# Heads of the fourth mixer computed already turned, both compressions on one tile, diagonal blocks moved by sums, and a new order for the mixers

## The reference, cut to what matters

```python
def nsa_compress(kv, pos_emb, w1, w2):          # first mixer: for keys, and again for values
    ...
    flat = (blocks + pos_emb.astype(jnp.float32)).reshape(B, G, n, CMP_BLOCK * d)
    return jax.nn.gelu(flat @ w1.astype(jnp.float32)) @ w2.astype(jnp.float32)

def hgrn2_chunkwise(q, k, v, log_f):             # second mixer
    ...
    attn = jnp.sum(qc[:, :, :, None, :] * decay * kc[:, :, None, :, :], axis=-1)

def chunk_attention(x, k_band, v_band, band_valid, w_q, rel_table, w_o):   # fourth mixer
    q = (x @ w_q).reshape(b, nc, CHUNK, B_HEADS, B_HEAD_DIM) * (B_HEAD_DIM ** -0.5)
    ...
    sc = jnp.einsum('bnqhd,bnkhd->bhnqk', q, k_band,
                    preferred_element_type=jnp.float32) + bias[:, None]
```

## Time and profile before

| | us |
|---|---|
| median of 3 runs | 1274.83 |
| lowest and highest | 1274.36, 1276.19 |
| the profiled execution, its own time | 1274.34 |
| its span, first to last instruction | 1272.5 |

### The profile page before, as it was taken

How to read it: one execution, slowest core, us unless ns; L and a number is a source line. 1 busy time by engine, 2 the same in 40 slices (tenths; PEclk the granted TensorE clock), 3 DMA queues, 4 the chain that set the end, 5 groups by cost and what they waited for, 6 DMA issues and landing times.

```text
span 1272.5 us, 20336 instructions
## 1 busy us (share of the span) xinstructions
PE 1256.7 (99%) x7562; PEld 1055.9 (83%) x7562; DVE 501.2 (39%) x1108; ACT 766.1 (60%) x1481; POOL 1029.1 (81%) x874
## 2 busy tenths in 40 slices
PE   8999999999999999999999999999999999999997
PEld 7877888888887887888888888888888888888886
DVE  3575423331168862333105665133203345233302
ACT  7656676654688877666445685365534565366631
POOL 6666789878977568988888877798889887699874
PEclk9999999999999999999999999999999999999999
DMA  8543566656654436666666545677565644567652
GB/s 284 159 133 108 158 209 217 194 166 185 183 163 134 134 94 206 195 187 189 178 194 195 162 150 148 198 213 218 184 196 174 224 149 136 162 215 224 202 171 82
DMA packets 63121, 224.96 MB, mean 177 GB/s; under 512 B 7344, under 2 KB 7984, under 8 KB 63024
## 3 DMA queue, kind: packets, MB, share of 16 engines
q1 hardware_dynamic: 62736, 223.57, 57.1%
q10 hardware_dynamic: 288, 0.10, 0.0%
HBM read 222.59 MB, written 1.05 MB: 176 GB/s over the span
## 4 chain that ended last, share of the span: by engine, by line
PE 94%; DVE 2%; POOL 2%; ACT 2%; DMA 1%; issue 1%; SPq 0%; DVEq 0%; ACTq 0%
PE G L1048 18%; PE G L1049 17%; PE G L1055 17%; PE G L1074 10%; PE A L1074 10%; PE A L1077 5%; PE G L1077 5%; POOL wlo L2328 1%; PE A L1179 1%; PE A L1103 1%; PE A L1215 1%; PE A L1239 1%; DMA X<-in_x 0%; PE A L1339 0%; PE A L1318 0%
## 5 line engine op out<-in xcount | busy, mean ns | idle before, releaser
L2328 POOL TENSOR_TENSOR wlo<-raw,whi 128x256 fp32r<-128x256 f32 (+2 forms) x866 | 1019.6, 1213 | 225.8 <-ACT whi L2028 224.8
L2028 ACT ACTIVATE whi<-raw 128x1024 fp32r<-128x1024 f32 x403 | 422.3, 1057 | 199.6 <-PE G L1055 145.0
L1048 PE MATMUL G<-whi,xx 128*128 128x512 f32 (+1 forms) x560 | 226.0, 404 | 0.5 <-DVE xx L1435 0.3
L1049 PE MATMUL G<-whi,xx 128*128 128x512 f32 (+1 forms) x560 | 217.1, 388 | 0.0
L1055 PE MATMUL G<-wlo,xx 128*128 128x512 f32 (+1 forms) x560 | 171.3, 388 | 0.0
L1074 PE MATMUL G<-xx,whi 128*128 128x512 f32 x576 | 144.7, 393 | 0.0
L1074 PE MATMUL A<-xx,whi 128*128 128x512 f32 x576 | 144.4, 393 | 0.0
L1048 PE MATMUL G<-whi,hh 128*128 128x512 f32 x352 | 137.6, 391 | 0.0
L1049 PE MATMUL G<-whi,hl 128*128 128x512 f32 x352 | 137.2, 390 | 0.0
L1048 PEld LDWEIGHTS G<-whi,xx 128*128 128x128 f32 x560 | 105.3, 188 | 24.9 <-issue 5.5
L1055 PEld LDWEIGHTS G<-wlo,xx 128*128 128x128 f32 x560 | 104.6, 188 | 22.4
(11 more groups left out here) (388 smaller groups left out, 1499.3 us busy)
## 6 DMA issues: line engine op xcount, KB each, us to landing
raw<-in_g SPq DMA_DIRECT2D x88, 512.0 KB, 3.9
raw<-in_u SPq DMA_DIRECT2D x88, 512.0 KB, 4.1
raw<-in_d SPq DMA_DIRECT2D x88, 512.0 KB, 4.0
raw<-in_w_h SPq DMA_DIRECT2D x32, 512.0 KB, 3.6
raw<-in_w_e SPq DMA_DIRECT2D x24, 512.0 KB, 3.9
raw<-in_w_a SPq DMA_DIRECT2D x24, 512.0 KB, 3.6
raw<-in_w_b SPq DMA_DIRECT2D x24, 512.0 KB, 3.7
raw<-in_w_eo SPq DMA_DIRECT2D x8, 512.0 KB, 3.6
```

Of the source, the lines that this page charges most:

```text
L1048: e.matmul(o, sh[:, kt, xs], whi[h][:, ws], start=u.first and j == 0, stop=False)
L1049: e.matmul(o, sl[:, kt, xs], whi[h][:, ws], start=False, stop=False)
L2028: e.activation(whi[c % NH][:, 0:n], raw[c % NR][:, 0:n], ACT.Copy).then_inc(s_hi, 1)
L2328: m = e.tensor_tensor(wlo[c % NH][:, i:j], raw[c % NR][:, i:j], whi[c % NH][:, i:j].bitcast(F), ALU.subtract)
```

## The change

It does five things. (1) The blocks of w_b are ordered v 0, qk 0 to qk 3, v 1, and q and k are computed in sixteen turned units of one chunk each, two heads on the 128 partitions (`turned_heads`); they use two banks in turn, an ACT copy (`QX`) and a DVE add (`QA`) put the halves together in `QTa` or `KTa`, and head n+2 waits for the add of head n. `KT`, `KA`, `KV` and the evictions of q and k leave the fourth mixer, which has 48 units instead of 64. (2) `CA` computes keys on the lower and values on the upper 64 columns of the array, in turn; the GELU runs once on 128 partitions, and `CF` and `CG` are one step each. (3) `DB` and the placing of the position embeddings (`MB`) use a `tensor_reduce` over an axis of one element instead of `tensor_copy`. (4) The side steps of all mixers stand in a new order. (5) In the first mixer the gates' buffer waits for one `CA`, not two.

```diff
+B_ORDER = (("v", 0), ("qk", 0), ("qk", 1), ("qk", 2), ("qk", 3), ("v", 1))
...
+                if st == 6 and B_ORDER[blk][0] == "qk":
+                    for j in range(4):
+                        ((c, kts),), at = feed(name, D, 128, at)
+                        units.append(Unit(st, ("h", 4 * B_ORDER[blk][1] + j), c, 0, kts, 128, 0, True, True))
+                    continue
...
+        def head_bank(n):
+            return G[0][:, 512 * (n % 2):512 * (n % 2) + 512]
+        def head_rest(n):
+            return PJ2[:, n % 2, 256 * (n // 2):256 * (n // 2) + 256]
...
+            def turned_heads(u):
+                _, n = u.blk
+                h, o = u.chunk % NH, head_bank(n)
+                before = B_ORDER.index(("qk", n // 4)) - 1
+                e.wait_ge(s_hi, u.chunk + 1)
+                if n % 4 > 1:
+                    half_added(n - 2)
+                elif B_ORDER[before][0] == "qk":
+                    half_added(4 * B_ORDER[before][1] + 2 + n % 4)
+                else:
+                    evicted(6, before, n % 4)
+                for kt in u.kts:
+                    e.matmul(o[:, :], whi[h][:, 128 * kt:128 * kt + 128], xx[:, kt, :], start=kt == 0, stop=False)
+                e.wait_ge(s_lo, u.chunk + 1)
+                for kt in u.kts:
+                    m = e.matmul(o[:, 0:256], wlo[h][:, 128 * kt:128 * kt + 128], xx[:, kt, 0:256], start=False,
+                                 stop=kt == u.kts[-1])
+                m.then_inc(s_unit, 1)
...
-                    wt = w1c[:, kind, 64 * m:64 * m + 64]
-                    o = e.matmul(tile[0:64, 0:45].rearrange("p (g i) -> p g i", g=3), wt, z, start=m == 0, stop=m == 15)
+                    for kind in range(2):
+                        z = Z[:, 3 * kind:3 * kind + 3, 2 * m:2 * m + 225:16]
+                        o = e.matmul(tile[64 * kind:64 * kind + 64, 0:45].rearrange("p (g i) -> p g i", g=3),
+                                     w1c[:, kind, 64 * m:64 * m + 64], z, start=m == 0, stop=m == 15)
...
-                    m = e.tensor_copy(mixed[rows, :, :, rows], blocks[rows])
+                    m = e.tensor_reduce(mixed[rows, :, :, rows], blocks[rows].unsqueeze(4), X_AX, ALU.add)
...
+            def half_add(key):
+                if j < 2:
+                    e.scalar_tensor_tensor(out=to, in0=head_bank(n)[:, 0:256], scalar=0.125, in1=head_rest(n), op0=ALU.mult,
+                                           op1=ALU.add).then_inc(S["QA"], 1)
+                else:
+                    e.tensor_tensor(to, head_bank(n)[:, 0:256], head_rest(n), ALU.add).then_inc(S["QA"], 1)
...
+            def half_copy(key):
+                _, n = key
+                e.wait_ge(s_unit, ENDS[6, ("h", n), 0])
+                e.activation(head_rest(n), head_bank(n)[:, 256:512], ACT.Copy,
+                             scale=0.125 if n % 4 < 2 else 1.0).then_inc(S["QX"], 1)
```

The new order of the fourth mixer around the turned heads (units 8 to 23), of the second mixer where the diagonal step and the decay products stand, and of the start:

```diff
+8: QX 0; QA 0
...
+12: QX 4; SC 0 0 @1; SC 0 1 @2; QA 4; MK 0 0; MK 0 1; EX 0 0; NW 0 0; LB 2
+13: QX 5; QA 5
+14: QX 6; QA 6; CPA 0 0; TR 0 0; EX 0 1
+15: QX 7; QA 7; AV 0 0
+16: NW 0 1; WH 0 0; QX 8; WL 0 0; SC 1 0 @0; QA 8; TBM 2; SC 1 1 @1; MK 1 0
+17: MK 1 1; TR 0 1; CPA 0 1; CPV 0 1; QX 9; QA 9; EX 1 1; QX 10
+18: LB 3; EX 1 0; QA 10
+19: TR 1 1; QX 11; NW 1 1; QA 11
+20: CPV 1 1; NW 1 0; QX 12; QA 12; WL 0 1; TR 1 0; CPA 1 1
...
-29: H4 0 1; H3 1 0; H4 1 0
-32: H4 1 1; GF 0; FB 2 @2
+30: H4 0 1; H4 1 0; HA 0 1; H3 1 1; H5 0 1; HA 1 0; GB 0 @2; GC 0; EV 3 1; H4 1 1
-35: FD 2; DB 0
+35: DB 0; FD 2
-38: H1 2 0 @1; H2 2 0; FF 2; T1 1 @0; TV 1; EV 4 0; FG 2; EV 4 1; TA 1
+38: H1 2 0 @1; H2 2 0; FF 2; T1 1 @0; TV 1; EV 4 0; FG 2; TA 1; EV 4 1
-42: H1 2 1 @0
+44: H1 2 1 @0; H5 2 0; GF 1; H1 3 1 @1; H1 3 0 @2
...
--1: -XT 0 0; -SQ 0 0; -XH 0 0; HI 0; -XL 0 0; -XT 0 1; LO 0; -XH 0 1; -XT 1 0
+-1: -XT 0 0; -SQ 0 0; -XH 0 0; HI 0; -XL 0 0; -XT 0 1; LO 0; -XT 1 0
-0: HI 1; -XT 1 1; -XL 0 1; -XH 1 0; HI 2
+0: HI 1; -XH 0 1; -XT 1 1; -XL 0 1; -SQ 0 1; HI 2; -XH 1 0
-18: CA 0 @2; CA 1 @0; CB 0; TT 2 @1; CE 0; TC 2; CB 1; EV 2 0; CD 0; CD 1; CE 1; CG 0; MK 0 0 1; MK 1 0 0
+18: CB 0; CE 0; EV 2 0; CD 0; TC 2; CG 0; MK 0 0 1
+19: CA 0 @0; TT 2 @1; QT 0 @2; MK 1 0 0
```

More of the change, by code:

```diff
@@ L139 @@
 A_AT = [(512 * i if kind == "qk" else 2048 + 512 * i, 512) for kind, i in A_ORDER]
-BLOCKS = {0: E_AT, 2: H_AT, 4: A_AT, 6: A_AT}
+B_AT = [(512 * i if kind == "qk" else 2048 + 512 * i, 512) for kind, i in B_ORDER]
+BLOCKS = {0: E_AT, 2: H_AT, 4: A_AT, 6: B_AT}
 QK_BLOCK = [A_ORDER.index(("qk", p)) for p in range(4)]
-V_BLOCK = [A_ORDER.index(("v", i)) for i in range(2)]
+V_BLOCK = {st: [order.index(("v", i)) for i in range(2)] for st, order in ((4, A_ORDER), (6, B_ORDER))}
 H_BLOCK = {pair: i for i, pair in enumerate(H_ORDER)}
@@ L580 @@
 70: RES 0 0; BN 0 0
[L581 removed]
+74: RES 0 1
+82: BN 0 1
 85: TBM 1
@@ new lines @@
+22: QX 14; QA 14
+23: SC 2 0 @0; SC 2 1 @2; QA 15; MK 2 0; QX 15; EX 2 0; MK 2 1; SC 3 0 @1
+24: NW 2 0
+25: EX 2 1; CPA 2 0; MK 3 0
+26: TR 2 0
+27: NW 2 1; EX 3 0; NW 3 0; EV 5 0
+28: CPV 2 1
+29: CPA 2 1; TR 2 1; WL 2 0
+30: EV 5 1; CPA 3 0; WH 2 0
+32: TR 3 0; WH 2 1; WH 3 0
+33: WL 2 1; MK 3 1; AV 2 0; AV 3 0; AV 2 1; SC 3 1 @0; NW 3 1; WL 3 0; RES 0 0
+35: EX 3 1
+42: TR 3 1; CPV 3 1; BN 0 0; RES 1 0; BN 1 0
+43: CPA 3 1; AG 0; WH 3 1; WL 3 1; AV 3 1; AP 0 0
+44: RS 0
+45: AP 1 0; XT 0 0; XH 0 0
@@ L631 @@
+46: XL 0 0
+47: RES 0 1; BN 0 1; XT 1 0
 """,
@@ L1033, in product @@
                         e.wait_ge(S["RO"], nth("RO", u.st, ROTATED[u.st, u.blk - 1], u.t))
+                    elif u.st == 6 and not wide and u.blk > 0:
+                        half_added(4 * B_ORDER[u.blk - 1][1] + 2 + u.t)
                     elif u.st % 2 == 0 and not wide and u.blk > 0:
@@ L1369, in qk_turn @@
                 lane_free("KT", key)
-                if st == 4:
-                    for t in range(2):
-                        e.wait_ge(S["RO"], nth("RO", st, p, t))
-                else:
-                    evicted(st, QK_BLOCK[p], 0, 1)
+                for t in range(2):
+                    e.wait_ge(S["RO"], nth("RO", st, p, t))
                 for t in range(2):
@@ L1528, in gelu_argument @@
                 tile, w = lane_of("CA", key)
-                x, u, bias = w[0][0:64, 0:30], tile[0:64, 64:94], w[0][0:64, 96:97]
+                x, u, bias = w[0][:, 0:30], tile[:, 64:94], w[0][:, 96:97]
                 k = -2.0 * (2.0 / np.pi) ** 0.5
                 e.wait_ge(S["CA"], nth("CA", *key))
-                e.tensor_copy(bias, tile[0:64, 30:31]).then_inc(s_dve, dv.up())
+                e.tensor_copy(bias, tile[:, 30:31]).then_inc(s_dve, dv.up())
                 own()
-                e.tensor_scalar(x, tile[0:64, 0:30], bias, None, ALU.add).then_inc(s_dve, dv.up())
+                e.tensor_scalar(x, tile[:, 0:30], bias, None, ALU.add).then_inc(s_dve, dv.up())
                 own()
@@ L1576, in place_positions @@
                 for kind, at_pos in enumerate((POSK, POSV)):
-                    m = e.tensor_copy(Z[:, 3 * kind + 2, 0:32:2], CP[:, at_pos:at_pos + 16])
+                    m = e.tensor_reduce(Z[:, 3 * kind + 2, 0:32:2], CP[:, at_pos:at_pos + 16].unsqueeze(2), X_AX, ALU.add)
                 m.then_inc(S["MB"], 1)
@@ L2161, in gelu_exp @@
                 tile, _ = lane_of("CA", key)
-                u = tile[0:64, 64:94]
+                u = tile[:, 64:94]
                 e.wait_ge(S["CB"], nth("CB", *key))
```

356 lines of the change are left out of this document (158 added, 198 removed), and 2 rows, old and new, of the table SIGNALS.

## The result

The kernel after takes 1266.36 us (median of 4 runs, 1265.78 to 1266.6) where the kernel before took 1274.7 on the same chip: ratio 0.9928, interval 0.9916 to 0.994. The forecast was 1269.1 us. The sign was right and the gain was forecast some 3 us too small.

A forecast was written before the change was run, and what follows sets the result against it. TensorE, busy 99%, bounds the kernel, so its stream's work sets the time. Terms -2.3 - 2.6 + 0.3 - 1.9 + 0.4 - 0.4 + 0.5 + 0.8 = -5.2 took 1274.34 to 1269.1 us; own range 1266.5 to 1272, wide 1266.0 to 1274.5.

The forecast's parts named there:

- Turned heads: Fourth mixer: dropping KT transposes saves 3.2 us and two interruptions 0.2, turned chunks cost 1.1 more; net -2.3 us.
- rival C: Fourth mixer, heads 4 to 15: TensorE waits for the half copies, kernel slower at 1281 us; chance 0.08.
- Compression: First mixer: 64 key and value records, alternating between column halves, take half of 5.19 us; -2.6 us.
- the second layer: First mixer: products of the compression's second layer wait for the chain with less cover; +0.3 us (0 to 1.1).
- Rival A: Compression: the two column halves don't run together, so the 2.6 us gain is lost, 1271.7 us; chance 0.12.
- Diagonal blocks: Second mixer: sums take 1.4 us instead of 5.0 for copies, ending TensorE's stall at the decay product; -1.9 us.
- given back: Second mixer: behind the removed stall, decay products come closer and a level product may wait; +0.4 us (0 to 1.9).
- The triple: Second mixer, unit 30: three level products in a row bring an issue wait; +0.8 us (0 to 1.4).
- Places: Each interruption of products by side work costs 0.09 us; 114 to 110 outside the fourth mixer, -0.4 us.
- Start: First mixer's start: split of chunk 1 goes first, delaying the second row tile's product; +0.5 us (0 to 1.06).
- Rival B: The new order removes one stall and makes others of 3 to 5 us, 1272 to 1274 us; chance 0.18.

The follow-up runs named there:

- e3: Kernel before with only the turned heads and the new order of the fourth mixer: 1272.17 us, ratio 0.9983.
- e4: Kernel after with all 32 compression products of keys ahead of the 32 of values, not alternating: 1268.47 us, ratio 0.9953.
- e1: Kernel before with only the diagonal blocks moved by one-element sums instead of copies, every order old: 1272.24 us, ratio 0.9981.
- e9: Kernel before with only the new order of the second mixer (units 8 to 79), diagonal blocks still copied: 1272.11 us, ratio 0.9972.
- e2: Kernel after with the diagonal blocks copied again instead of summed, new order kept: 1268.03 us, ratio 0.9946 to the kernel before.
- e13: Kernel after with the first of three level products of the second mixer's unit 61 moved one unit earlier: 1266.74 us, ratio 0.9933.
- e15: Kernel after with three edits: old order of the start, first level product of unit 61 one unit earlier, last norm's loads eight chunks later: 1265.49 us, ratio 0.9925.
- e6: Kernel after with the three old lines of the order at the start of the first mixer: 1267.03 us, ratio 0.9931.
- e10: Kernel after with the two 512 KB loads of the last norm's scale and shift issued eight chunks later in the fourth mixer: 1265.77 us, ratio 0.9931.
- e14: Kernel after with 4 instead of 8 small matmuls at its very start: 1267.9 us, ratio 0.9943.
- e16: Kernel before with the whole first mixer of after and the diagonal blocks by sums, other orders old: 1269.09 us, ratio 0.995.
- e7: Kernel after with the last of three level products of the second mixer's unit 61 moved one unit later: 1267.1 us, ratio 0.9934.
- e5: Kernel before with only the compression side by side, its steps standing where those of the keys stood: 1280.44 us, ratio 1.0045.
- e12: Kernel before with the whole first mixer of after, all else old, diagonal blocks still copied: 1277.16 us, ratio 1.0019.
- e8: Kernel after with 32 instead of 8 small matmuls at its very start: 1271.14 us, ratio 0.9968.

## Why the prediction was wrong in size

- Turned heads: forecast -2.3, measured -2.3 (e3). The half copies never held TensorE; rival C didn't come.
- Compression: records -2.6 forecast, -2.45 measured, and the 0.3 us of the second layer are not there. Rival A is ruled out by e4.
- Diagonal blocks: the stall went, -1.9 forecast, and the sums alone gave -2.0 (e1). The step that failed was its cause. I read the 5.00 us as the copy's price and took the order of DVE as given, but the new order of the stage ended the stall with the copies too (e9, e2). The likely line of it is the swap of `DB` with `FD 2` at unit 35; the swap alone was not run. And nothing was given back: +0.4 forecast, 0 measured.
- The triple: +0.8 forecast, 0 measured. The analogy took the neighbourhood of a wait for its cause.
- Places: the largest error, and a term that I gave no bounds. The forecast's own range has all its bounded terms at their best at 1266.5 us, and the kernel was still a little faster. (Its upper end, 1272, was added up wrongly: with every bound at its worst it is 1275, and 1272.6 with rival A's left aside.) I priced an interruption at 0.09 us, the delay of the first product behind it, and left out the delay ahead of the side step and behind its last record. e13 shows one whole place, a single level product between two units:

```profile
443.98 0.61 PE L1059 MATMUL G<-wlo,xx 128*128 128x512 f32 x2
444.53 0.25 PE L1358 MATMUL A<-W 128*32 128x64 f32 x2
...
445.26 0.50 PE L1052 MATMUL G<-whi,xx 128*128 128x512 f32 x1
445.60 0.39 PE L1053 MATMUL G<-whi,xx 128*128 128x512 f32 x1
```

 The last product starts at 444.21 (the second of two from 443.98), the second one behind at 445.60: 1.39 us. Two plain distances of 0.227 are in it, and the level product itself, which takes 0.58 us when another follows it in after (446.49 to 447.07, the two starts of their L1358 rows). 1.39 - 0.45 - 0.58 = 0.36 us. Stage 2 says the same: less the pause, e13 and e15 have 148.75 and 148.77 us where after, e6, e10 and e14, with one place fewer, have 148.31 to 148.37, so 0.40; and the old order with sums, two places more, has 149.07, so 0.36 each. Stage 0 agrees: e16 has three places fewer than before and 3.3 us less, of which 2.45 are the records' and 0.1 a wait of 0.13 us for `W` that went, while the new start costs 0.4 more; the 1.1 us left are some 0.37 a place. But it is no price for every place. The rows of before show one of four 128x128 transposes, and the products ahead of `KT`:

```profile
974.79 0.62 PE L1055 MATMUL G<-wlo,xx 128*128 128x512 f32 x2
975.25 0.60 PE L1103 MATMUL A<-CN,X 128*128 128x128 f32 x4
975.61 0.48 PE L1048 MATMUL G<-whi,xx 128*128 128x512 f32 x1
975.92 0.39 PE L1049 MATMUL G<-whi,xx 128*128 128x512 f32 x1
...
1011.90 0.62 PE L1055 MATMUL G<-wlo,xx 128*128 128x512 f32 x2
```

 Counted the same way, four transposes take 975.92 - 975.02 = 0.90 us and the eight of `KT` 1013.46 - 1012.12 = 1.34. The four more cost 0.44, or 0.11 each, so with the two plain distances off nothing is left for the place. In stage 4 one place more cost 0.1 us: 110.05 to 110.08 us in e2, e4, e6, e7, e13 and e15, against 109.94 to 110.03 with the old order; the 110.34 of after holds a wait besides (a row of 0.08 us, 0.3 between starts). So outside the fourth mixer five places fewer gave 1.8 us and one more took 0.1, where the forecast had 0.4.
- Start: +0.5 forecast, 0.4 measured at the second tile's product, some 0.3 in the stage (e6). The 0.7 us between starts at the low half (26.3 us) were not forecast.
- Sum by the measured terms: -2.5 (heads in e3's stage 6 with its two places) - 2.45 - 2.0 - 1.8 + 0.1 (the places) + 0.3 + 0.7 + 0.3 (the wait in stage 4) = -7.35 us, against -7.7 in the span. The missing 0.35 is mostly stage 6, which fell by 2.8 us in after and by 2.5 in e3; that stage differs so from profile to profile.
- So the mechanism was right, that TensorE's own stream sets the time, and the sizes were off: places (-0.4, measured -1.7), the triple (+0.8, measured 0), the part given back (+0.4, measured 0) and the second layer (+0.3, measured 0). That the miss is only 3 us is in part luck: the two waits not forecast took 1.0 us back.

Rival B (the new order makes stalls of its own) didn't come in after. Its mechanism is real, though: the compression in the old order made waits of 1.4, 2.9 and 5.9 us. I had given "+0.3, nothing else moves" to an edit whose real risk was to shift POOL against DVE.

## What to carry to other kernels

On a kernel bound by one engine, count the places where its stream is interrupted and price each kind of them by its own rows, from the last main instruction ahead to the second one behind, not by one delay of one kind. Read a duration that varies (here 0.2 to 8.5 us for one copy) as a wait, and look at the shortest of the same line before pricing it: an operation that can wait on another engine's ports makes every edit upstream risky, and replacing it is worth most where the order doesn't hide it. Before explaining a stall by its neighbours, look for the same stall in an edited kernel and count instructions to it.

## What the runs showed of the hardware

- A float32 SBUF to SBUF copy or tensor_scalar on DVE waits while POOL works without a break: 0.20 to 8.47 us for 32x128, 0.17 to 4.73 for 128x24. Sometimes it gets in between two POOL operations (0.68 us, before), sometimes it waits until POOL stands still (e5, e12). What decides is open. A tensor_reduce of the same block took 0.26 to 0.28 us in all of twelve kernels.
- Instructions arrive in loads of 16 KB, one per 124 matmul records (that this queue is TensorE's is my inference from the pauses). A pause followed 145 level-product matmuls in 1.7 us (after), 184 in 2.1 (e8), and a shorter one 89 in 1.1 (e13), and in seventeen traces it ended 2.2 to 2.4 us after a load had started.
- A place with side work between 512-column products costs nothing beside its work where the work is 128x128 transposes (0.90 us for four, 1.34 for eight, before), and 0.36 us where it is a level product of 32x32 matmuls (e13).
- Products of 45 columns on alternating halves of the array's columns start 0.043 us apart; on the same half 0.076 to 0.081.
- The 24 matmuls added in e8 while TensorE seemed to wait for x moved the first product from 9.23 to 14.05 us. The warm-up rows of after and e8 show it, and the idle time there was 1.3 us only:

```profile
1.05 3.78 PE L1117 MATMUL G<-PJ 128*128 128x128 f32 x16 [1.05 <-DVE PJ L1427]
```
```profile
1.05 10.08 PE L1117 MATMUL G<-PJ 128*128 128x128 f32 x64 [1.05 <-DVE PJ L1427]
```
